# Expert rows weighted on TensorE and added to their tokens team by team, one set of squares for two norms, and products of constants in TensorE's waits

## The reference

```python
y = einsum('tef,efd->td', silu(t @ w1) * (t @ w3) * gates, w2)   # two gates per token are not 0
x = x + gate2 * y
x = rms_norm(x, final_g)                     # end of the first block
hn = rms_norm_2(x, ln_gain)                  # start of the second block
rms_norm(x, g) = x * rsqrt(mean(x * x) + 1e-6) * g
```

## Time and profile before

| | |
|---|---|
| median of 3 runs | 3461.1 us (3459.1 to 3470.57) |
| the profiled execution, its own time | 3463.11 us |
| its span | 3460.6 us |
| time around the span | 2.5 us |
| PE busy, weight loads busy | 83%, 70% |
| DVE, ACT, POOL busy | 34%, 34%, 49% |
| mean granted clock of PE | 0.91 |
| HBM moved | 696 MB, mean 201 GB/s |

### The profile page before, as it was taken

One profiled execution on the slowest core, in us unless ns is written; L12 is line 12 of the kernel. 1 busy time (PEld: TensorE's weight loads), 2 busy tenths in 40 slices (PEclk: granted clock), 3 DMA queues, 4 the chain that ended last, 5 costly groups with the idle time before them and its releaser, 6 DMA issues.

```text
span 3460.6 us, 52768 instructions
## 1 busy us (share of the span) xinstructions
PE 2885.3 (83%) x20704; PEld 2416.4 (70%) x20704; DVE 1169.6 (34%) x1616; ACT 1189.2 (34%) x1360; POOL 1686.3 (49%) x1290
## 2 busy tenths in 40 slices
PE   6999899898998987566776449877899988889898
PEld 1677688787898876322332148777789987879898
DVE  1487821124352333300000053366611234432335
ACT  1223333333544322201111124455544444444343
POOL 0000067676767765000000119654479975559897
PEclk8999999899999999688998669898999998889999
DMA  9432247375434767399999915433335543325443
GB/s 393 171 114 103 103 168 296 144 274 206 157 133 157 283 256 278 148 409 387 369 392 385 389 49 184 142 111 105 108 134 182 182 155 119 112 104 187 157 169 134
DMA packets 100898, 696.28 MB, mean 201 GB/s; under 512 B 11840, under 2 KB 15680, under 8 KB 17088
## 3 DMA queue, kind: packets, MB, share of 16 engines
q1 hardware_dynamic: 83088, 602.97, 46.6%
q10 hardware_dynamic: 15408, 74.85, 5.7%
q0 software_dynamic: 2272, 16.52, 1.2%
HBM read 774.25 MB, written 14.42 MB: 228 GB/s over the span
## 4 chain that ended last, share of the span: by engine, by line
PE 64%; DMA 13%; DVE 10%; ACT 7%; issue 3%; POOL 2%; SPq 1%; ACTq 1%; DVEq 0%; POOLq 0%
PE acc L569 51%; PE wk L569 10%; DMA ring<-in_moe 8%; DMA side_buf<-in_ada 2%; DMA stage<-in_ada 2%; ACT w_hi L1189 2%; PE acc L627 2%; POOL w_lo L542 2%; ACT L1189 1%; DVE yl L1729 1%; SPq L492 1%; DVE C_z L1732 1%; DVE rms_red L1741 1%; DVE C_sm L1729 0%; ACT hb L1189 0%
## 5 line engine op out<-in xcount | busy, mean ns | idle before, releaser
L542 POOL TENSOR_TENSOR w_lo<-stage,w_hi 128x512 fp32r<-128x512 f32 x1268 | 1668.7, 1348 | 1159.7 <-PE acc L569 615.3
L569 PE MATMUL acc<-xh,w_hi 128*128 128x256 f32 x3568 | 912.9, 294 | 29.9 <-DVE xl L1729 22.3
L569 PE MATMUL acc<-xl,w_hi 128*128 128x256 f32 x3568 | 899.6, 290 | 0.0
L569 PEld LDWEIGHTS acc<-xh,w_hi 128*128 128x128 f32 x3568 | 713.6, 200 | 73.3 <-issue 57.1
L569 PEld LDWEIGHTS acc<-xl,w_hi 128*128 128x128 f32 x3568 | 712.9, 200 | 0.7
L1189 ACT ACTIVATE w_hi<-stage 128x2048 fp32r<-128x2048 f32 x317 | 603.9, 1907 | 39.7 <-DMA stage<-in_main 35.3
L569 PE MATMUL acc<-xh,w_lo 128*128 128x256 f32 x3568 | 476.7, 287 | 0.0
L569 PEld LDWEIGHTS acc<-xh,w_lo 128*128 128x128 f32 x3568 | 452.2, 195 | 3.2 <-issue 2.3
L557 POOL DMA_DIRECT2D y_rows<-X_ysb x12 | 6.6, 552 | 560.4 <-ACT X_ysb L1189 560.4
L569 PE MATMUL acc<-h,stage 128*128 128x256 f32 x1024 | 233.8, 385 | 2.9 <-ACT h L1189 2.9
L569 PE MATMUL acc<-ring,xg 128*32 128x512 f32 x1024 | 150.0, 732 | 89.4 <-DMA ring<-in_moe 88.7
(11 more groups left out here) (455 smaller groups left out, 3641.3 us busy)
## 6 DMA issues: line engine op xcount, KB each, us to landing
stage<-in_main SPq DMA_DIRECT2D x317, 1024.0 KB, 4.8
ring<-in_moe SPq DMA_DIRECT2D x192, 1024.0 KB, 10.8
side_buf<-in_ada ACTq DMA_DIRECT2D x64, 1024.0 KB, 5.0
over_lo<-in_moe ACTq DMA_DIRECT2D x48, 1024.0 KB
over_hi<-in_moe ACTq DMA_DIRECT2D x42, 1024.0 KB
stage<-in_ada SPq DMA_DIRECT2D x32, 1024.0 KB, 8.6
stage<-in_sb SPq DMA_DIRECT2D x32, 1024.0 KB, 4.7
y_rows<-X_ysb POOLq DMA_DIRECT2D x11, 1024.0 KB, 9.8
```

What stands on the lines that cost most here:

```text
L542: last = pool.tensor_tensor(w_lo[:, k % 2, cs], stage[:, k, cs], w_hi[:, k, cs].bitcast(F32), ALU.subtract)
L569: return pe.matmul(o, w, r, start=start, stop=stop)
```

## The change

**Rows to tokens.** POOL's writes to `y_rows` and its four gathers go. For each team, DVE makes a matrix `X["pg"]` (`weigh`: five instructions) that has the gate of token t at the row that t has in this team, and 0 elsewhere; PE transposes it with `hid` in `turn`, DVE copies it to `X["gT"]`, and PE multiplies `ysb` with it (`combine`, 16 fp32 matmuls of 256 columns into the banks `wk`). DVE adds each result to `x` (`collect`, 16 instructions). `combine(p-1)` stands after `turn(p)`, at overflow positions after `gather`. `down(p)` waits until `collect(p-1)` has emptied `wk`; ACT's copy to `ysb` waits for `combine` instead of the write to DRAM. `up` and `turn` wait for `gT_ready` in place of `hT_ready`. Two copies of slot numbers (`slots`) go from the routing.

**Norms.** ACT squares `x` tile pair by tile pair as the last `collect` leaves it; PE sums each pair twice, with `ones` and with the squared gains `g2` as weights (`squares`, 32 fp32 matmuls of 256 columns, in turns with the last `combine`). From the two sums, s for x and s2 for x times `g_fin`, DVE makes the variance of the second norm, so that `hb` is scaled from `x` at once and the product of the gains, `gg`, is applied. DVE normalizes `x` for the residual afterwards, with 16 instructions.

**Products of constants.** `spin` multiplies `ones` with `ident` (fp32, 128 columns) into the upper half of an `acc` bank whose result nobody reads: 30 before `glu`, 24 before `p_s5`, 36 before `wout`, 30 and 20 around the sum before `router`, 36 before `kv`, 40 before `wout2`; and in the loops 10 in `stage_b` (3 rounds), 12 in `stage_c` (7 rounds), 5 in `stage_d` (7 rounds), each ahead of the wait named above.

```diff
@@ -551,15 +552,6 @@
         pool.wait_ge(chunk_done, BASE["kv"])
         pool.memset(over_lo[:], 0.0).then_inc(over_clear, 1)
         pool.memset(over_hi[:], 0.0).then_inc(over_clear, 1)
-        for p, team in enumerate(TEAMS):
-            pool.wait_ge(moe_ev, p + 1)
-            rows = CAP * len(team)
-            pool.dma_start(y_rows[team[0] * CAP:team[0] * CAP + rows, :], X["ysb"][0:rows, :]).then_inc(y_out, 16)
-        pool.wait_ge(y_out, 16 * len(TEAMS))
-        for w in range(2):
-            for h in range(2):
-                pool.indirect_dma_start(yg[:, w, h, :], None, y_rows[:, :],
-                                        bass.IndirectOffsetOnAxis(ap=slots[:, w, h:h + 1], axis=0)).then_inc(yg_in, 16)
         each(pool, BASE["kv"], NMAIN - BASE["kv"], low)
 
...
+        def spin(times, n):
+
+            pe.wait_ge(evac_done, n - 3)
+            k = n % 4 if isinstance(n, int) else None
+            for _ in range(times):
+                mm(acc[:, k, T:T + P], ones[:], ident[:])
+
...
+        spin(30, BASE["glu"])
+        spin(24, BASE["p_s5"])
+                    spin_in(10, base_b, g, 2)
+        spin(36, BASE["wout"])
+        spin(30, BASE["router"])
+        spin(20, BASE["router"])
+        spin(36, BASE["kv"])
+                    spin_in(12, base_c, g)
+                    spin_in(5, base_d, g)
+        spin(40, BASE["wout2"])
...
@@ -939,7 +952,7 @@
             team = TEAMS[p]
             pe.wait_ge(hT_ready, p + 1)
             if p:
-                pe.wait_ge(moe_ev, p)
+                pe.wait_ge(comb_used, 8 * p)
             for c in range(2):
                 w = [arrive(p, a, 4 + c) for a in range(len(team))]
...
             for c in range(2):
-                last = pe.transpose(acc[:, turn_bank(p), c * P:c * P + rows], X["hid"][0:rows, c * P:(c + 1) * P], ident[0:rows, 0:rows])
+                pe.transpose(acc[:, turn_bank(p), c * P:c * P + rows], X["hid"][0:rows, c * P:(c + 1) * P], ident[0:rows, 0:rows])
+            pe.wait_ge(pg_ready, p + 1)
+            for h in range(2):
+                last = pe.transpose(acc[0:rows, turn_bank(p), T + h * P:T + (h + 1) * P], X["pg"][:, h, 0:rows], ident[:])
             last.then_inc(turn_done, 1)
+
+        def combine(p):
+
+            rows = CAP * len(TEAMS[p])
+            pe.wait_ge(moe_ev, p + 1)
+            pe.wait_ge(gT_ready, p + 1)
+            for i in range(8):
+                if i >= 4:
+                    pe.wait_ge(comb_used, 8 * p + i - 3)
+                for j in range(2):
+                    t = 2 * i + j
+                    last = mm(wk[:, i % 4, j * T:(j + 1) * T], X["ysb"][0:rows, t * P:(t + 1) * P], X["gT"][0:rows, p % 2, :])
+                last.then_inc(comb_done, 1)
+                if p == len(TEAMS) - 1 and i >= 3:
+                    squares(i - 3)
+
+        def squares(i):
+
+            if not i:
+                pe.wait_ge(gains_ready, 1)
+            pe.wait_ge(sq_done, i + 1)
+            for t in (2 * i, 2 * i + 1):
+                mm(acc[:, 0, 0:T], ones[:], sq[:, t, :], t == 0, t == DT - 1)
+                last = mm(acc[:, 1, 0:T], R["g2"][:, t:t + 1].to_broadcast([P, P]), sq[:, t, :], t == 0, t == DT - 1)
+            if i == 7:
...
                 down(p - 1)
                 turn(p)
                 gather(p // 2 + 1)
+                combine(p - 1)
                 down(p)
             else:
                 up(p)
@@ -973,20 +1016,14 @@
                 if p and p - 1 not in OVER_TEAMS:
                     down(p - 1)
                 turn(p)
+                if p:
+                    combine(p - 1)
         down(len(TEAMS) - 1)
-
-        pe.wait_ge(dg_ready, 1)
-        pe.wait_ge(yg_in, 64)
-        pe.wait_ge(moe_ev, len(TEAMS))
-        for t in range(DT):
-            if t >= 4:
-                pe.wait_ge(ot_used, 16 + t - 3)
-            for h in range(2):
-                for w in range(2):
-                    last = mm(wk[:, t % 4, h * P:(h + 1) * P], yg[:, w, h, t * P:(t + 1) * P], dg[:, w, h, :], w == 0, w == 1)
-            last.then_inc(comb_done, 1)
-        channel_sum(3)
-        channel_sum(4)
+        combine(len(TEAMS) - 1)
+
+        for i in range(5, 8):
+            squares(i)
+        spin(36, BASE["kv"])
 
 
         for c in range(4):
...
             if p:
-                act.wait_ge(y_out, 16 * p)
+                act.wait_ge(comb_done, 8 * p)
             fn(X["ysb"][0:rows, :], wk[0:rows, :, :].rearrange("p a b -> p (a b)"), ACT.Copy).then_inc(moe_ev, 1)
 
...
             high(*slot(n))
-        rms_root(3)
-        rms_affine(3, x, lambda t: col("g_fin", t))
-        rms_root(4)
-        affine_split(4, 48, lambda t: col("g_ln2", t))
+        for i in range(8):
+            if i < 4:
+                act.wait_ge(comb_used, 8 * (len(TEAMS) - 1) + i + 1)
+            else:
+                act.wait_ge(ot_used, 16 + 4 * (i - 3))
+            fn(sq[:, 2 * i:2 * i + 2, :], x[:, 2 * i:2 * i + 2, :], ACT.Square).then_inc(sq_done, 1)
+        act.wait_ge(rms_var, 3)
+        fn(rms_red[:], rms_red[:], ACT.Sqrt).then_inc(rms_sd, 1)
+        fn(rinv[:], rinv[:], ACT.Sqrt).then_inc(x_sd, 1)
+        affine_split(3, 32, lambda t: R["gg"][:, t:t + 1])
 
 
...
 
+        def weigh(p):
+
+            q = TEAM_ORDER[p]
+            for w, to_ in ((0, X["pg"]), (1, R["pk2"])):
+                for h in range(2):
+                    ts(to_[:, h, :], R["iota"][:, 0:P], R["off"][:, w, h, q:q + 1], ALU.is_equal,
+                       R["gw"][:, w, h:h + 1], MUL).then_inc(pg_half, 1)
+            dve.wait_ge(pg_half, 4 * p + 4)
+            tt(X["pg"][:], X["pg"][:], R["pk2"][:], ADD).then_inc(pg_ready, 1)
+
+        def collect(p):
+
+            dve.wait_ge(comb_used, 8 * p)
+            for i in range(8):
+                dve.wait_ge(comb_done, 8 * p + i + 1)
+                for j in range(2):
+                    t = 2 * i + j
+                    ins = stt(x[:, t, :], wk[:, i % 4, j * T:(j + 1) * T], mod[:, 80 + t:81 + t], x[:, t, :], MUL, ADD)
+                if p == len(TEAMS) - 1 and i >= 4:
+                    ins.then_inc(ot_used, 4)
+                else:
+                    ins.then_inc(comb_used, 1)
+
...
+            cp(X["gT"][0:rows, p % 2, :], acc[0:rows, turn_bank(p), T:2 * T]).then_inc(gT_ready, 1)
             if more and p in OVER_TEAMS:
                 pick_rows(p // 2 + 2)
-
-        for w in range(2):
-            for h in range(2):
-                ins = ts(dg[:, w, h, :], ident[:], R["gw"][:, w, h:h + 1], MUL)
-        ins.then_inc(dg_ready, 1)
-        dve.wait_ge(mod_ready, 7)
+            if p + 1 < len(TEAMS):
+                weigh(p + 1)
+            if p:
+                collect(p - 1)
+        collect(len(TEAMS) - 1)
+        dve.wait_ge(comb_used, 8 * (len(TEAMS) - 1) + 4)
+
+        dve.wait_ge(ot_used, 16 + 16)
+        dve.wait_ge(rms_sum, 3)
+        ts(rinv[:], acc[:, 0, 0:T], 1.0 / D, MUL, EPS, ADD)
+        ts(rms_red[:], acc[:, 1, 0:T], 1.0 / D, MUL).then_inc(vo_d, 1)
+        dve.wait_ge(vo_d, 2)
+        stt(rms_red[:], rinv[:], EPS, rms_red[:], MUL, ADD).then_inc(rms_var, 1)
+        dve.wait_ge(rms_sd, 3)
+        dve.reciprocal(rms_red[:], rms_red[:]).then_inc(rms_inv, 1)
+        dve.wait_ge(rms_inv, 3)
+        for g in range(4):
+            gs = slice(4 * g, 4 * g + 4)
+            tt(hb[:, gs, :], x[:, gs, :], rms_red[:].unsqueeze(1).to_broadcast([P, 4, T]), MUL).then_inc(rms_scaled, 1)
+        split_lo(hb, 8)
+        dve.wait_ge(x_sd, 1)
+        dve.reciprocal(rinv[:], rinv[:]).then_inc(x_inv, 1)
+        dve.wait_ge(x_inv, 1)
         for t in range(DT):
-            dve.wait_ge(comb_done, t + 1)
-            stt(x[:, t, :], wk[:, t % 4, 0:T], mod[:, 80 + t:81 + t], x[:, t, :], MUL, ADD).then_inc(ot_used, 1)
-        dve.wait_ge(ot_used, 16 + 16)
-        rms(3, x)
-        dve.wait_ge(rms_affine_done, 48)
-        rms(4, x)
-        split_lo(hb, 8)
+            stt(x[:, t, :], x[:, t, :], vec[:, VC["g_fin"] + t:VC["g_fin"] + t + 1], rinv[:], MUL, MUL)
 
 
```

More of the change, by code:

```diff
@@ L238, in build @@
     X = {}
-    for n, s, dt in [("ysb", [P, D], F32), ("s", [P, T], F32), ("hid", [P, T], F32), ("hT", [P, 2, P], F32),
+    for n, s, dt in [("ysb", [P, D], F32), ("s", [P, T], F32), ("hid", [P, T], F32), ("hT", [P, 2, P], F32), ("gT", [P, 2, T], F32),
+                     ("pg", [P, 2, P], F32),
                      ("pick_at", [P, 2, GROUP * CAP], F32R)]:
@@ L390, in build @@
     ring_in = [nc.alloc_semaphore(f"ring_in{k}") for k in range(RING)]
[L391 removed]
+    pg_half = nc.alloc_semaphore("pg_half")
+    pg_ready = nc.alloc_semaphore("pg_ready")
+    gT_ready = nc.alloc_semaphore("gT_ready")
     pick_half = nc.alloc_semaphore("pick_half")
[L393 to L394 removed]
+    comb_used = nc.alloc_semaphore("comb_used")
+    gains_ready = nc.alloc_semaphore("gains_ready")
+    sq_done = nc.alloc_semaphore("sq_done")
+    x_sd = nc.alloc_semaphore("x_sd")
+    x_inv = nc.alloc_semaphore("x_inv")
```

(16 more changed lines are left out.)

25 lines of the change are left out of this document (10 added, 15 removed).

## The result

The changed kernel takes 3416.6 us (median of four runs, 3408.5 to 3423.1), the kernel before 3461.9 beside it: a ratio of 0.986, 95% interval 0.984 to 0.989. The prediction was 3408 in a range of 3380 to 3440. The profiled execution took 3416.85 us (span 3415.1) against 3463.1, so it is 46.3 us shorter where the sum of the prediction has 55.1.

The account below looks back on a forecast made before the run. PE was taken to bound the dense stages, DMA the expert stage outside overflow rounds, with nothing overlapping in the seam. 3463.1 - 41.6 (seam) + 17 (experts) - 30 (constant products) - 0.3 (routing copies) = 3408 us, range 3380 to 3440.

Parts of the forecast that it names:

- The seam: From the last down to kv: 41.6 us in place of 83.2, so -41.6, bounds -25 and -44.
- the term that the copies stand in the way: In the seam, ACT's four w_hi copies are queued ahead of the first Square: 7.3 us, ending at 9.2.
- Rival 4: In the seam the 48 products run at 1.2 GHz: -25 there, 3425 us in all; chance 0.12.
- The expert stage: Combines exposed in overflow rounds, less the POOL writes that go: +17 us, bounds -22 and +92.
- I take 1.08: In the expert stage, DVE adds one pair of a combine in 1.08 us, between 0.84 and 1.2.
- Products of constants: Fillers in PE's waits cost nothing and return the slow start after the wait: -30 us, bounds 0 and -44.
- So I take half of 7 x 2.3: 8: NSA: filling part of the wait keeps the clock up in about half of the possible gain: 8 us returned.
- shorter than the waits that they stand in, so they cost nothing: All constant products fit in PE's waits, for example 2.7 of 5.8 us in NSA and 1.1 of 3.2 in Fox.
- Fox: ... 7: Fox: five of seven rounds start slow, 1.4 us each, with 2.1 left idle: 7 us returned.
- mLSTM's 7: mLSTM: constant products return some 3 us for each of three rounds, of which 7 were taken.
- the large waits: Seven large waits filled with constant products: up to 2.4 us each, 12 together, two thirds taken: 8.
- Rival 1: The clock isn't held where an idle rest is left: the 30 us shrink to 3, 3435 in all; chance 0.18.

Follow-up runs that it names:

- copies_between: The changed kernel with ACT's four w_hi copies of kv put between its Squares instead of ahead of the first; 3406.6 us, 0.985 of the kernel before.
- no_products: The changed kernel with every call of spin and spin_in left out; 3430.0 us, 0.992 of the kernel before.
- fill_waits: The changed kernel with 25 constant products per NSA round in place of 12, and 14 in fox in place of 5; 3400.5 us, 0.984 of the kernel before.
- fill_both: fill_waits with 12 more constant products ahead of NSA's second wait, for C_z; 3393.0 us, 0.980 of the kernel before.
- same_again: The changed kernel with no edit, executed once more; 3424.9 us in a single execution.

## Why the prediction was right, and where it was off

The forecast of 3408 is 9 us under the 3416.6 measured. Of its three large terms two were right and one failed; a stage that it put at 0 came 5 us shorter by chance, which covers part of that.

- **The seam**, -41.6: -43.2. Of its parts, the copies wait 0.55 us twice for their loads (1.4 predicted), the first Square came when expected, and the products ran at full pace but for the first few. copies_between confirms the term that the copies stand in the way. Rival 4 (products at 1.2 GHz throughout) is out: 19.0 us for 40 of them is 0.48 each, where half the clock would be 0.89. (Its -25 is the price of 40 products; all 48 would give -20.)
- **The expert stage**, +17: +13.9. The mechanism was right (79.7 for an overflow round against 81.0 and 79.2, 76.8 for the third against 75.6; by parts 0.2, 17.6 and -3.9 us before, in and behind the three rounds, against 4, 19.3 and -6). Two sizes were off and offset each other. "I take 1.08" for DVE's pair measured 0.79, under the lower end of 0.84, so a combine holds PE for 10.0 and not 11.9 at an overflow position, and all combines cost 36.5, not 46. A write cost 2.0 and not 2.6, 22.3 in place of 29; that some fell where PE sets the pace is the likely reason, and was expected of this run, but isn't shown. PE waits there for `x` (0.83 us) and for DVE's last addition (1.81), as said.
- **Products of constants**, -30: -18 to -20 by no_products. Here the steps failed. "So I take half of 7 x 2.3: 8" for NSA measured +3.2, for two reasons. The first is "shorter than the waits that they stand in, so they cost nothing": the call ahead of the first head meets no wait and costs 2.7 us (1.1 in fox), and the last head's wait has no call. That PE doesn't wait there could be read from the trace of the kernel before. The second is the clock: an idle rest of 3.1 us lowered it in five of the six rounds that have one (0.70 to 0.80 us for the first product in place of 0.48), and in four of seven it fell at the wait for `C_z`, which I had used as evidence that 2.85 us are harmless. In the kernel before they were harmless in the rounds in which the clock had fallen at the wait ahead; fill_waits and fill_both show that filling the first wait moves the fall there. Against the kernel before itself NSA lost only 1.1 us, since its first round was 2.3 longer there (45.2 us) than in no_products (42.9), which has the same code in NSA. "Fox: ... 7" measured 3.7: one of seven rounds was shorter by 3, for behind the wait of 2.1 us that is left, made longer by the delay of `E_rm`, the clock still fell. mLSTM's 7 measured 7.0, the large waits 2.4 to 8.8 against 8. Rival 1 was right in NSA, nearly so in fox (five of six rests of 2.1 us were followed by a fall), and wrong in mLSTM, where behind rests of 1.8 us the granted clock stayed at 1.00.
- **The last stage**, 0: -5.2. DVE's four `hb` took 13.32 us beside POOL's `w_lo` in the kernel before and 9.12 in the changed one:

```profile
3333.80 9.12 DVE L1777 TENSOR_TENSOR hb<-merged,rinv 128x1024 f32<-128x1024 f32 x4
3328.86 17.88 POOL L543 TENSOR_TENSOR w_lo<-stage,w_hi 128x512 fp32r<-128x512 f32 x11
```

```profile
3374.11 13.32 DVE L1729 TENSOR_TENSOR hb<-merged,rinv 128x1024 f32<-128x1024 f32 x4
3369.17 13.78 POOL L542 TENSOR_TENSOR w_lo<-stage,w_hi 128x512 fp32r<-128x512 f32 x11
```

  Either DVE's first `hb` waits 9.9 us until POOL's queue is empty and the others take 1.2, or the two take turns at 2.3 a piece. The long form came in the profiled executions of six of the twelve runs, in same_again among them, which is the changed kernel itself. So it is no part of the change but chance, and the forecast was lucky in it: without it the profiled execution is 14 us short of the sum. By stages, those that only the products of constants changed gave back 11.0 us in place of 30, and the seam and the expert stage 4.7 more than forecast. (That 11.0 and the 18 to 20 of no_products differ is mostly the scatter before the router.)

## What to carry to other kernels

In a loop with more than one idle wait, fill all of them, not the longest one, and price a held clock from a run in which all are filled: in NSA the longest alone returned 0.5 us of a round, both together 2.0. A wait that did no harm so far may only have stood behind one that had done it already. Check for each filler, the first and last round above all, that it meets a wait: one that meets none costs its full length (2.7 us in NSA, 5.5 with 25 products). Look for a small VectorE instruction whose time differs between rounds beside a running GpSimd, and put what TensorE waits for ahead of it. And before calling the path's new work hidden or exposed, take it out and put the old work back, each alone: here 36.5 and 22.3 us gave the net of 14 that neither shows.

## What the runs showed of the hardware that was not expected

- The start of a 0.34 us VectorE instruction relative to GpSimd's, 0.12 us earlier or later, is worth 25 us over seven rounds (278.8 against 253.7 us of fox): in six rounds 1.05 us in the instruction and 0.12 ahead of it, the rest the clock behind the longer wait. A second one, `E_qks`, takes 0.69 or 1.80 us by a difference of 0.02.
- A fall of the clock that was kept off at one wait came at the next, of 2.85 us (`C_z` at 1.36 in fill_waits against 0.88), which had cost nothing while the wait ahead of it took the fall.
- Two large two-operand instructions of VectorE and GpSimd either take turns (2.3 us each) or one waits for the other's whole queue (9.9 us), in executions of the same code (13.34 against 9.12 us for four).
